# Six SBUF buffers of a four-layer transformer kernel start 128 bytes later

## The chip, the cores and the metric

The kernel runs on one core of one Trainium2 chip. The metric is the device time of one execution in microseconds, the median of several runs.

## The reference

Two blocks of two layers each work on 256 tokens of 1024 features, all in float32. Cut to what matters here:

```
# first block
z = rmsnorm(x, g) @ a_w_in;  q, k, v, q_mem = split(z)       # rope on q and k
x = x + concat(diff_attention(q, k, v), memory_attention(q_mem, mem)) @ a_w_out
x = x + relu(rmsnorm(x, g) @ a_w_up)**2 @ a_w_down
kv = rmsnorm(x, kv_norm) @ w_kv;  z = rmsnorm(x, g) @ b_w_in
x = x + concat(moba_attention(...), memory_attention(...)) @ b_w_out
x = x + relu(rmsnorm(x, g) @ b_w_up)**2 @ b_w_down
x = rmsnorm(x, final_norm)
# second block
h = x + rmsnorm(stick_breaking_attention(rmsnorm(x, g) @ sb_w_qkv) @ sb_w_o, g)
h = h + rmsnorm(conv_ffn(rmsnorm(h, g)), g)                  # up, causal conv of width 3,
h = h + rmsnorm(forgetting_attention(q, k, v, fcum) @ fox_w_o, g)   # gelu(gate) * up, down
h = h + rmsnorm(conv_ffn(rmsnorm(h, g)), g)
```

`fcum` is the running sum of the log of a forget gate, which comes from the product with `w_f`, 16 columns padded to 128.

## The kernel before

The activations lie with features on the partitions: `X` is 128 x 8 x 256, feature tile by token. The work is a list of 18 products, `GEMMS`: `mem_a`, `in_a`, `mem_b`, `out_a`, `up_a`, `down_a`, `in_b`, `out_b`, `up_b`, `down_b`, `in_sb`, `out_sb`, `up_sb`, `down_sb`, `in_fox`, `out_fox`, `up_fox`, `down_fox`. I call the stretch of the trace in which one is computed a stage.

**The weights.** SyncE streams them in units of 128 x 1024 (128 x 768 or 640 in `down_sb` and `down_fox`) into `raw`, a ring of four slots. ScalarE rounds a unit to the float32r type into `w_hi` (L815), VectorE subtracts to get the rest into `w_lo` (L1128). A unit holds up to eight k-tiles of 128 x 128.

**The activations** are split the same way. `h1_hi`, `h1_lo` and `h2_hi`, `h2_lo` hold the normed input of a product (L819 on ScalarE writes hi, L1172 on VectorE writes lo); `a_hi`, `a_lo` hold the hidden layer of an MLP, `o_hi`, `o_lo` the attention output. Every k-tile costs three matmuls of 256 columns, a triple:

```
nc.tensor.matmul(dst, w_hi[:, slot, w], src_hi[:, at + k, :], start=begin, stop=False)   # L497
nc.tensor.matmul(dst, w_hi[:, slot, w], src_lo[:, at + k, :], start=False, stop=False)   # L498
last = nc.tensor.matmul(dst, w_lo[:, slot, w], src_hi[:, at + k, :], start=False,        # L499
```

The first operand of `matmul` after the destination is stationary, loaded by a weight load of its own; the second moves. L467 to L469 in `query_key_tile` are the same triple for the fused projections, L517 to L519 the same for the first tiles of `up_sb` and `up_fox`. Sources: `h2` for `up_a`, `up_b`, `up_sb`, `up_fox` and for the memory tiles in `in_a`; `h1` or `h2` by tile in `in_b` and `in_fox`; `h1` in `in_sb`; `o` for all `out_` and `a` for all `down_` stages. The value columns of the fused projections (L447 to L449) have it the other way round: `h1` is stationary, `w` moves, 512 or 256 columns at a time. The forget gate's product (L729 to L731) has `wf_hi` and `wf_lo` stationary and `h1` moving.

**H** is a work buffer with several uses: attention outputs before their norm, outputs before a post-norm, and in the MLPs `u_buf`, `m_buf` and `gate` are views of it:

```
u_buf = H[:, 0:4, :]
m_buf = H[:, 4:6, :]
gate = H[:, 6:8, :]
```

In `up_sb` and `up_fox`, tile by tile: VectorE scales a bank into `u_buf` (L1226), ScalarE starts `conv_buf` with one tap (L876), GpSimd makes another tap's product in `m_buf` (L1555), VectorE adds a tap (L1232), GpSimd adds `m_buf` (L1561) and, for every pair, multiplies `gate` with it into `prod` (L1566); ScalarE rounds `prod` into `a_hi` (L865), VectorE makes `a_lo` (L1192). `ZM` holds the memory input and later the memory keys, `mv_tok` the memory values, `wf_hi` and `wf_lo` the split of `w_f`.

**Order.** All engines run their own program; counters (semaphores) tie them. For a matmul unit TensorE waits for `lo_ready` of its weights and `tile_out` of the bank it reuses, nothing else in the steady state.

**Where buffers lie.** `sb(name, shape)` gives buffers one after another in the order of the calls, each beginning where the one before ends, small ones rounded up to 32 bytes per partition. Two calls whose result is not kept only take room: `lead_h1`, 48 x 4 = 192 bytes, and `lead_ident`, 192 bytes. Counted from the start of `raw`, `w_hi` begins at 16384, `w_lo` at 32768, `X` at 49152, `h1_hi` at 57536, `h1_lo` at 65728, `h2_hi` at 73920, `h2_lo` at 82112, `H` at 90304, `ZM` at 98496, `mv_tok` at 106688, `wf_hi` at 110784, `wf_lo` at 114880. A tile of 256 tokens is 1024 bytes, a k-tile of weights 512.

Of the kernel before, what the change touches and what calls it, by code (L numbers as in the profile page):

```python
# [22 lines left out]
P = 128  # L23
# [89 lines left out]
def build_program(nc, ins, out):  # L113
# [6 lines left out]
    with ctx:  # L120
        def sb(name, shape, dt=f32):
            return ctx.enter_context(nc.sbuf_tensor(name, shape, dt))
# [10 lines left out]
        h1_hi = sb("h1_hi", [P, KT, TOK], f32r)  # L133
        h1_lo = sb("h1_lo", [P, KT, TOK], f32r)
        h2_hi = sb("h2_hi", [P, KT, TOK], f32r)
        h2_lo = sb("h2_lo", [P, KT, TOK], f32r)
        H = sb("H", [P, KT, TOK])
        ZM = sb("ZM", [P, KT, TOK])
        mv_tok = sb("mv_tok", [P, 2, 2, MEM_W])
        wf_hi = sb("wf_hi", [P, KT, P], f32r)  # L140
        wf_lo = sb("wf_lo", [P, KT, P], f32r)
        sb("lead_ident", [P, 48])
        ident = sb("ident_sb", [P, P])
        ones = sb("ones_sb", [P, TOK])
        rope_c = sb("rope_c_sb", [P, TOK])
# [1544 lines left out]
```

## Time and profile before

| | us |
|---|---|
| median of 3 runs | 1337.02 |
| lowest and highest | 1335.78, 1337.67 |
| the profiled execution's own time | 1337.67 |
| its span, first to last instruction | 1335.9 |

The span is the part of the profiled execution that the trace shows; the time has 1.8 us more around it. The profile's engines are PE (TensorE matmuls), PEld (its weight loads), DVE (VectorE), ACT (ScalarE) and POOL (GpSimd). A matmul's duration runs to its modelled end and overlaps the next one's, so the starts, not the durations, tell how fast they follow each other. PEclk is the TensorE clock granted, 1.00 for full and 0.50 for half.

### The profile page before, as it was taken

How to read it: one execution, taken by the hardware profiler on the slowest of the kernel's cores; microseconds unless marked ns; L12 is line 12 of the kernel's file. 1: busy time of each engine (PE TensorE's matmuls, PEld its weight loads, DVE VectorE, ACT ScalarE, POOL GpSimd, SP SyncE). 2: the span in 40 equal slices, each digit the busy share in tenths (PEclk: the TensorE clock that was granted, in tenths of full speed). 3: DMA queues.
4: the chain of work that ended last, by engine and by line, in shares of the span. 5: the costliest groups of instructions: out<-in, count | busy, mean ns of one | idle time of the engine just before them, and what ended most of it. 6: DMA issues, size and time to landing. Idle time of an engine off the chain costs nothing. (4 is left out here: it accounts for less than half of the span.)

```text
span 1335.9 us, 29554 instructions
## 1 busy us (share of the span) xinstructions
PE 1246.4 (93%) x9952; PEld 1177.5 (88%) x9952; DVE 947.2 (71%) x1545; ACT 734.2 (55%) x1307; POOL 477.9 (36%) x465
## 2 busy tenths in 40 slices
PE   7988999999997999999997889998999999899896
PEld 7977999999985999999885779998979978899896
DVE  6598677656597677545699479997475756899844
ACT  6556554444554555444656566665465556666642
POOL 2231255300022355210222258885130004888711
PEclk9999899999998999999998799999989989999998
DMA  7544365566543456656443225555645433555472
GB/s 273 174 143 127 111 205 189 178 196 204 177 142 96 157 189 192 202 188 190 157 127 111 82 93 179 173 182 151 186 136 174 127 95 112 158 181 171 141 207 85
DMA packets 63287, 212.40 MB, mean 159 GB/s; under 512 B 7793, under 2 KB 8945, under 8 KB 62833
## 3 DMA queue, kind: packets, MB, share of 16 engines
q1 hardware_dynamic: 63216, 211.50, 50.3%
q8 instruction: 39, 0.64, 0.2%
q14 instruction: 32, 0.25, 0.1%
HBM read 207.28 MB, written 1.05 MB: 156 GB/s over the span
## 5 line engine op out<-in xcount | busy, mean ns | idle before, releaser
L1128 DVE TENSOR_TENSOR w_lo<-raw,w_hi 128x1024 fp32r<-128x1024 f32 (+2 forms) x408 | 508.9, 1253 | 144.8 <-ACT w_hi L815 144.8
L815 ACT CAST w_hi<-raw 128x1024 fp32r<-128x1024 f32 (+2 forms) x408 | 408.2, 1004 | 251.6 <-PE bank L499 166.3
L497 PE MATMUL bank<-h_hi,w_hi 128*128 128x256 f32 x1168 | 328.6, 281 | 12.2 <-DVE w_lo L1128 11.3
L498 PE MATMUL bank<-h_lo,w_hi 128*128 128x256 f32 x1168 | 324.0, 277 | 0.0
L499 PE MATMUL bank<-h_hi,w_lo 128*128 128x256 f32 x1168 | 323.9, 277 | 0.0
L1497 POOL TENSOR_TENSOR sumsq<-sumsq,square 128x256 f32<-128x256 f32 x107 | 95.6, 893 | 471.5 <-ACT square L827 287.2
L497 PE MATMUL bank<-a_hi,w_hi 128*128 128x256 f32 x896 | 251.3, 281 | 11.0 <-DVE w_lo L1128 9.3
L498 PE MATMUL bank<-a_lo,w_hi 128*128 128x256 f32 x896 | 250.5, 280 | 0.0
L499 PE MATMUL bank<-a_hi,w_lo 128*128 128x256 f32 x896 | 250.4, 279 | 0.0
L497 PEld LDWEIGHTS bank<-h_hi,w_hi 128*128 128x128 f32 x1168 | 220.2, 189 | 19.3 <-issue 18.6
L499 PEld LDWEIGHTS bank<-h_hi,w_lo 128*128 128x128 f32 x1168 | 220.4, 189 | 0.0
L498 PEld LDWEIGHTS bank<-h_lo,w_hi 128*128 128x128 f32 x1168 | 220.1, 188 | 0.1
L497 PEld LDWEIGHTS bank<-a_hi,w_hi 128*128 128x128 f32 x896 | 170.4, 190 | 12.4 <-DVE w_lo L1128 10.1
L498 PEld LDWEIGHTS bank<-a_lo,w_hi 128*128 128x128 f32 x896 | 170.4, 190 | 0.0
L499 PEld LDWEIGHTS bank<-a_hi,w_lo 128*128 128x128 f32 x896 | 169.8, 190 | 0.0
L467 PE MATMUL bank<-h_hi,w_hi 128*128 128x256 f32 x512 | 147.6, 288 | 0.0
L468 PE MATMUL bank<-h_lo,w_hi 128*128 128x256 f32 x512 | 143.3, 280 | 0.0
L469 PE MATMUL bank<-h_hi,w_lo 128*128 128x256 f32 x512 | 143.1, 280 | 0.0
L1541 POOL TENSOR_TENSOR prod<-H 128x256 f32<-128x256 f32 x64 | 89.2, 1393 | 84.8 <-DVE H L1203 84.8
L467 PEld LDWEIGHTS bank<-h_hi,w_hi 128*128 128x128 f32 x512 | 97.4, 190 | 5.1 <-issue 4.9
L1555 POOL TENSOR_TENSOR H<-H,conv_sb 128x256 f32<-128x256 f32 x88 | 97.1, 1103 | 9.8 <-DVE H L1226 7.7
L469 PEld LDWEIGHTS bank<-h_hi,w_lo 128*128 128x128 f32 x512 | 97.2, 190 | 0.0
(154 smaller groups left out, 2123.6 us busy)
## 6 DMA issues: line engine op xcount, KB each, us to landing
raw<-in_w_up_sb SPq DMA_DIRECT2D x44, 512.0 KB, 3.4
raw<-in_w_up_fox SPq DMA_DIRECT2D x44, 512.0 KB, 3.4
raw<-in_w_up_a SPq DMA_DIRECT2D x32, 512.0 KB, 3.4
raw<-in_w_down_a SPq DMA_DIRECT2D x32, 512.0 KB, 4.7
raw<-in_w_up_b SPq DMA_DIRECT2D x32, 512.0 KB, 3.4
raw<-in_w_down_b SPq DMA_DIRECT2D x32, 512.0 KB, 4.4
raw<-in_w_in_sb SPq DMA_DIRECT2D x24, 512.0 KB, 3.6
raw<-in_w_in_fox SPq DMA_DIRECT2D x24, 512.0 KB, 4.3
```

The source lines that it names most:

```text
L467: nc.tensor.matmul(dst, w_hi[:, slot, w], src_hi[:, k, :], start=k == 0, stop=False)
L468: nc.tensor.matmul(dst, w_hi[:, slot, w], src_lo[:, k, :], start=False, stop=False)
L469: last = nc.tensor.matmul(dst, w_lo[:, slot, w], src_hi[:, k, :], start=False, stop=k == KT - 1)
L497: nc.tensor.matmul(dst, w_hi[:, slot, w], src_hi[:, at + k, :], start=begin, stop=False)
L498: nc.tensor.matmul(dst, w_hi[:, slot, w], src_lo[:, at + k, :], start=False, stop=False)
L499: last = nc.tensor.matmul(dst, w_lo[:, slot, w], src_hi[:, at + k, :], start=False, stop=end)
L815: nc.scalar.copy(w_hi[:, slot, 0:k * P], raw[:, slot, 0:k * P]).then_inc(hi_ready, 1)
L1128: nc.vector.tensor_tensor(w_lo[:, slot, 0:k * P], raw[:, slot, 0:k * P], w_hi[:, slot, 0:k * P].bitcast(f32), ALU.subtract).then_inc(lo_re ...
L1497: nc.gpsimd.tensor_tensor(sumsq[:], sumsq[:], square[:, b, :], ALU.add).then_inc(sum_done, 1)
L1541: nc.gpsimd.tensor_tensor(prod[:, b % 2, :], u_buf[:, b, :], u_buf[:, b, :], ALU.mult).then_inc(prod_ready, 1)
L1555: nc.gpsimd.tensor_tensor(m_buf[:, b % 2, :], u_buf[:, b % 2, :], conv[:, layer, 0, bass.ds(i * 4 + b, 1)].broadcast_to([P, TOK]), ALU.mul ...
```

## The change

One spacer of 128 bytes per partition is put ahead of `h2_lo`, and the later spacer `lead_ident` is made 128 bytes shorter. So `h2_lo`, `H`, `ZM`, `mv_tok`, `wf_hi` and `wf_lo` start 128 bytes later; all buffers ahead of them and all from `ident_sb` on stay. The instructions are the same.

```diff
         h2_hi = sb("h2_hi", [P, KT, TOK], f32r)
+        sb("lead_h2_lo", [P, 32])
         h2_lo = sb("h2_lo", [P, KT, TOK], f32r)
         H = sb("H", [P, KT, TOK])
         ZM = sb("ZM", [P, KT, TOK])
         mv_tok = sb("mv_tok", [P, 2, 2, MEM_W])
         wf_hi = sb("wf_hi", [P, KT, P], f32r)
         wf_lo = sb("wf_lo", [P, KT, P], f32r)
-        sb("lead_ident", [P, 48])
+        sb("lead_ident", [P, 16])
         ident = sb("ident_sb", [P, P])
```

## Rows read from the trace of the kernel before

**Rows 1.** The cores view (span, mean granted clock); busy time from the page.

```profile
core 0: 1335.9 us, clock 0.966
...
PE 1246.4 (93%) x9952; PEld 1177.5 (88%) x9952; DVE 947.2 (71%) x1545; ACT 734.2 (55%) x1307; POOL 477.9 (36%) x465
```

**Rows 2.** Windows: length, busy and (count) PE, PEld, DVE, ACT, POOL; PEclk, DMA.

```profile
164.00:251.00 87.00, 86.70 (x764) 86.45 (x762) 63.54 (x97) 46.26 (x68) 44.12 (x33) 1.00 0.62 195
...
435.00:462.00 27.00, 27.00 (x228) 27.00 (x227) 19.99 (x26) 15.12 (x25) 9.10 (x8) 0.98 0.43 139
...
745.00:772.00 27.00, 26.22 (x205) 25.00 (x205) 10.56 (x10) 13.56 (x27) 5.21 (x7) 0.91 0.44 136
772.00:922.00 150.00, 139.73 (x1127) 134.81 (x1125) 131.69 (x174) 93.90 (x157) 122.03 (x124) 0.98 0.48 150
922.00:981.00 59.00, 57.89 (x478) 57.89 (x479) 28.80 (x33) 30.39 (x46) 5.19 (x7) 0.97 0.68 195
...
1265.00:1336.00 71.00, 57.78 (x481) 56.81 (x481) 32.34 (x42) 28.97 (x47) 9.38 (x11) 0.94 0.48 142
```

**Rows 3.** Timeline (start, length), weight loads, up_a (41 rows) and down_a (42).

```profile
199.89 0.19 PEld L497 LDWEIGHTS bank<-h_hi,w_hi 128*128 128x128 f32 x1
...
204.42 0.19 PEld L498 LDWEIGHTS bank<-h_lo,w_hi 128*128 128x128 f32 x1
...
299.85 0.19 PEld L497 LDWEIGHTS bank<-a_hi,w_hi 128*128 128x128 f32 x1
...
304.49 0.19 PEld L499 LDWEIGHTS bank<-a_hi,w_lo 128*128 128x128 f32 x1
```

**Rows 4.** The same timeline in down_sb (40 rows) and out_b (39 rows).

```profile
949.83 0.19 PEld L498 LDWEIGHTS bank<-a_lo,w_hi 128*128 128x128 f32 x1
...
954.42 0.19 PEld L498 LDWEIGHTS bank<-a_lo,w_hi 128*128 128x128 f32 x1
...
439.93 0.19 PEld L499 LDWEIGHTS bank<-o_hi,w_lo 128*128 128x128 f32 x1
...
444.40 0.19 PEld L498 LDWEIGHTS bank<-o_lo,w_hi 128*128 128x128 f32 x1
```

**Rows 5.** The same timeline, the forget gate's product (23 rows).

```profile
1014.33 0.19 PEld L730 LDWEIGHTS bank<-h_lo,wf_hi 128*128 128x128 f32 x1
...
1016.96 0.19 PEld L731 LDWEIGHTS bank<-h_hi,wf_lo 128*128 128x128 f32 x1
```

**Rows 6.** The same timeline, the value product's 256-wide part in in_a (39 rows).

```profile
43.99 0.19 PEld L448 LDWEIGHTS bank<-w_lo,h_hi 128*128 128x128 f32 x1
...
48.47 0.19 PEld L447 LDWEIGHTS bank<-w_hi,h_hi 128*128 128x128 f32 x1
```

**Rows 7.** Down_sb at half the granted clock: window, then timeline (13 rows).

```profile
924.20:927.20 3.00, 3.00 (x16) 3.00 (x15) 2.33 (x3) 2.24 (x5) 0.62 (x1) 0.50 0.70 183
...
924.46 0.33 PEld L498 LDWEIGHTS bank<-a_lo,w_hi 128*128 128x128 f32 x1
...
927.02 0.33 PEld L498 LDWEIGHTS bank<-a_lo,w_hi 128*128 128x128 f32 x1
```

**Rows 8.** Windows of two successive pairs of tiles in up_sb, columns as in rows 2.

```profile
836.37:842.39 6.02, 5.72 (x48) 5.53 (x49) 5.51 (x8) 3.82 (x7) 5.28 (x6) 1.00 0.56 174
842.39:848.36 5.97, 5.92 (x48) 5.72 (x49) 5.49 (x8) 3.81 (x7) 5.22 (x6) 1.00 0.51 176
```

**Rows 9.** The chain that ended last, within up_sb: start, length, what.

```profile
849.13 0.65 POOL conv_buf L1561
...
850.00 1.45 POOL prod L1566
```

**Rows 10.** Two source lines of VectorE: duration ns min/median/max, first and last start.

```profile
L1354 DVE SCALAR_TENSOR_TENSOR H<-H,subln_s,n_buf x6: 479/480/484, 110.2 to 139.4; 128x256 f32<-128x256 f32 x6
...
L1434 DVE SCALAR_TENSOR_TENSOR X<-X,gains_sb,rstd x8: 471/474/958, 634.7 to 643.1; 128x256 f32<-128x256 f32 x8
```

**Rows 11.** The tile view of H, its last step on GpSimd, columns as in rows 10.

```profile
L1566 POOL TENSOR_TENSOR prod<-H,conv_buf x44: 727/1440/1601, 796.9 to 1263.7; 128x256 f32<-128x256 f32 x44
```

## The prediction

> **What bounds the kernel now.** I read the cores view first: one core, span 1335.9 us, mean granted TensorE clock 0.966 [rows 1]. The page's first part gives the engines: TensorE is busy 93% and its weight loads 88%, VectorE only 71%. The windows by stage then separate two kinds of stage [rows 2]. In up_a, out_b and down_sb TensorE is busy for 86.7 of 87, 27.0 of 27 and 57.9 of 59 us, nearly all of it at the full granted clock: there the time is set by how fast matmuls follow each other (down_a, up_b, down_b, the other out stages and down_fox are of this kind too). In up_sb TensorE is idle for 10 of 150 us, and VectorE (131.7) and GpSimd (122.0) are as good as full; up_fox is the same.
>
> For a change of addresses the busy time says too little, because a matmul's duration in the trace overlaps its neighbours'. The spacing of the starts is what counts. The timeline of weight loads alone (one load per matmul) gives it: first and last row of an unbroken stretch, divided by the number of steps. In up_a 40 steps take 204.42 - 199.89 = 4.53 us, 113.3 ns each, and in down_a 41 steps take 4.64 us, 113.2 ns [rows 3]. The same loop in down_sb takes 4.59 us for 39 steps, 117.7 ns, and in out_b 4.47 us for 38, 117.6 ns [rows 4]; out_sb and down_fox go at that pace too. So one loop, on operands placed alike, has two stable paces 4.4 ns apart. I call them the quick and the slow pace. Which one a stretch has is settled soon after TensorE starts again from a gap.
>
> Two other matmul groups are placed differently. Take addresses as distances from the start of raw. The buffers w_hi and w_lo sit at 0 modulo 512 bytes; all of h1, h2, o and a at 192. In the ordinary loop the moving operand (h, o or a) is therefore 192 ahead of the stationary one (w). In the forget-gate product (L729 to L731) both are at 192, distance 0: 22 steps take 1016.96 - 1014.33 = 2.63 us, 119.5 ns [rows 5]. In the value product (L447 to L449) w moves and h1 is stationary, distance 0 - 192, which is 320 modulo 512: its 256-wide part takes 48.47 - 43.99 = 4.48 us for 38 steps, 117.9 ns [rows 6]. The pace thus seems to hang on where the two operands lie relative to each other, though these groups differ from the loop in other ways as well.
>
> **The change part by part.** No instruction, wait, semaphore or DMA is added or removed. What changes is where six buffers lie: h2_lo, H, ZM, mv_tok, wf_hi and wf_lo each start 128 bytes later, at 320 instead of 192 modulo 512. The second spacer is 128 bytes shorter, so ident_sb and all after it stay. What stays relative is as important: h2_hi, h1, w, a and o are untouched.
>
> *h2_lo on TensorE.* It is the moving operand of the second matmul of each triple (L498, L468, L518) in up_a, up_b, up_sb, up_fox and in part of the fused projections. Its distance from w becomes 320, that of the value product. No row shows that distance in this loop. The cost is bounded from both sides. From above: the whole stream takes the value product's pace. up_a and up_b have 32 tiles of 8 triples each, 512 triples or 1536 matmuls, times 4.4 ns = 6.8 us. If the slow pace is then carried on without a gap into down_a and down_b (8 tiles of 32 k-tiles each, 2 x 768 matmuls), that is another 6.8 us. A nearer value is that only the matmul that reads h2_lo pays: 512 x 4.4 ns = 2.3 us. Nothing is lost if the distance doesn't matter, or if 192 and 320, which are 64 bytes to either side of a multiple of 256, are worth the same. From below: the quick pace is not the floor. Where the granted clock is 0.50 (its 1.2 GHz level) the loop takes 213.3 ns a step, 12 steps in 927.02 - 924.46 = 2.56 us [rows 7]; half of that at the full clock is 106.7, against the 113.3 of [rows 3], so a better distance could give back up to 6.6 ns. On 512 matmuls that is 3.4 us, and on all 1536 of up_a and up_b 10 us. I take the middle between nothing and one in three, 1.2 us, because two of the three matmuls in each triple keep their distance.
>
> *The same in up_sb and up_fox* (44 tiles each): costed at nothing. The two windows of [rows 8] are successive pairs of tiles, 48 matmuls each. The first is at the quick pace for most of its length, the second wholly at the slow one (its TensorE busy time is 5.92 against 5.72 us), and they take 6.02 and 5.97 us. What sets a pair is the chain in [rows 9]: conv_buf on VectorE, conv_buf and prod on GpSimd, a_hi, then the next w_lo. 48 matmuls need 5.44 us quick and 5.65 us slow, so there are at least 0.3 us of cover. Were it gone, the cost would be 2 x 352 x 4.4 ns = 3.1 us for one in three.
>
> *The fused projections.* 32 triples of the memory tiles in in_a, and 64 each in in_b and in_fox, read h2_lo. One in three paying is 160 x 4.4 ns = 0.7 us at most, and these stages have TensorE gaps, so I take nothing.
>
> *H, ZM, mv_tok and wf.* H is read and written by the chain of up_sb and up_fox. Do addresses matter to VectorE? The same form at 128x256 takes 479 to 484 ns when both inputs lie at 192 (H and n_buf, L1354), and 471 at the least with X at 0 and rstd at 64 (L1434) [rows 10]: 8 ns apart. One such step per pair on the chain and 44 pairs give 0.4 us either way. For GpSimd I see only durations that include waiting for VectorE: prod 727 to 1601 ns, median 1440 [rows 11]. With the same 2% on its 0.65 and 1.45 us it would be 44 x 0.042 = 1.8 us either way; I take 0. wf is read by 24 matmuls: at best 24 x (119.5 - 113.3) ns = 0.15 us back, taken as 0. ZM and mv_tok are used by a few tens of small operations, nothing.
>
> The sum: 1.2 us on the profiled execution's 1337.67 us, that is its span of 1335.9 us and 1.8 us around it, or 1338.9. It is the slowest of three; on the median 1337.02 it gives 1338.2 us.
>
> The Trainium skill speaks to this on its page "SBUF — State Buffer", section "Who interferes with whom": TensorE has two independent read ports, one for the moving operand and one for weights, and it and ScalarE never wait on anyone. By that rule the sum is 0. The 119.5 against 113.3 ns of [rows 5] and [rows 3] do not fit it easily, and so I leave it a part of my forecast and not the whole. The same page, in its specifications, says that SBUF works in 16-byte lines; 128 bytes is eight of them, so no access comes to lie across more lines, and no run here shows that.
>
> **The rivals.**
> *The distance counts for the whole stream* (slower). One late read per triple shifts the loads behind it, and the triple settles at the slow pace, as every triple of out_b and down_sb does. It speaks for this that a stretch is wholly quick or wholly slow, never a third of it, and that the value product stays at 117.9. It speaks against it that the value product also switches banks and uses one stationary operand twice. Price: 6.8 us for up_a and up_b, 13.6 us if it carries on to down_a and down_b, giving 1343.8 to 1350.6 us. It decides once the mean spacing in up_a is over 115 ns.
>
> *The moved h2_lo breaks the slow pace, or the starts fall out well* (faster). In four long stretches the slow pace now costs: out_b, out_sb, down_sb and down_fox. Their windows hold 228 + 205 + 478 + 481 = 1392 matmuls [rows 2], of which some 1320 follow at it once each stage has got going: 1320 x 4.4 ns = 5.8 us. Each is entered from a gap, and a start that is a few ns different can fall to the quick pace. All four give 1331.2 us; with the 3.4 us above, 1327.8. Against: none of these four reads h2_lo, so it takes a knock-on, and the three runs lie within 1.9 us, so the paces seem to repeat from run to run. It decides once two of the down and out stages turn quick.
>
> *Nothing at all happens*: 1337.0 us. For it speaks that 192 and 320 lie equally far from 256, and it lies inside the forecast's own case.
>
> **How the numbers follow.** 0.2% is 2.7 us, about what a measurement of this kernel can tell from no change. The forecast's case, between nothing and one matmul in three, spans 1337.0 to 1339.3 us; with a pace or two falling out otherwise in the short stretches its own range is 1334.5 to 1340. I give it 0.42. The whole stream slow: 0.29, plus 0.04 for long stretches turning slow by themselves. Faster, by a better pace or by better starts: 0.25. So faster 0.25, same 0.42, slower 0.33. The range runs from 1330.5 (nearly all four slow stretches turned quick) to 1346.5 (up_a, up_b and half of what may carry on).
>
> **What the profile afterwards would show.** First the spacing in up_a and up_b: 113.3 ns for no effect, about 114.7 for one in three, 117.7 for the rival. Then the same in down_a and down_b, where nothing moved. The pair time in up_sb and up_fox stays at 5.99 us, or H matters. The spacing of the forget-gate product tells by itself whether distance counts: there wf moves from 0 to 384, and only placement changes. DVE and ACT durations stay as they are. The prediction is wrong if up_a's pace moves by more than 2 ns, or if stages whose operands were not moved change pace by themselves and add up to more than 2.7 us.

## The result and the profile after

The changed kernel takes 1347.62 us (median of 6 runs, 1343.56 to 1350.45), the kernel before beside it 1335.02 us (6 runs, 1331.48 to 1337.67). The ratio is 1.0087, with a 95% interval from 1.0066 to 1.0107. It is slower; the forecast was 1338.2 us, and the range ended at 1346.5. The profiled execution of the changed kernel took 1344.47 us, its span is 1342.6 us.

The added spacer moves every line number of the kernel by one: L497 to L499 of before are L498 to L500 here. The windows of the changed kernel's trace, columns as in [rows 2] (up_a, down_a, up_b, down_b, then up_sb and up_fox from their first to their last weight load):

```profile
161.00:251.00 90.00, 89.80 (x761) 89.54 (x760) 64.00 (x97) 45.76 (x67) 43.42 (x33) 1.00 0.58 188
253.00:343.00 90.00, 90.00 (x767) 90.00 (x765) 50.84 (x55) 41.08 (x54) 7.42 (x9) 1.00 0.58 190
462.00:552.00 90.00, 89.79 (x761) 89.53 (x760) 64.07 (x96) 45.91 (x68) 43.42 (x33) 1.00 0.58 189
554.00:645.00 91.00, 90.47 (x766) 90.07 (x765) 42.91 (x42) 36.25 (x42) 8.81 (x9) 1.00 0.60 189
...
790.80:927.40 136.60, 131.65 (x1059) 127.62 (x1059) 122.39 (x163) 87.01 (x143) 112.53 (x112) 0.99 0.46 149
1128.10:1264.80 136.70, 132.22 (x1059) 127.74 (x1059) 122.26 (x163) 87.03 (x143) 110.70 (x112) 0.99 0.46 149
```

Up_a holds 761 matmuls in 90 us where 87 us held 764 before [rows 2], at the same full granted clock and with TensorE busy throughout. So the matmuls follow each other more slowly and nothing else waits. The timeline of weight loads shows it; first and last row of an unbroken stretch in up_a (40 rows), down_a (40), up_b (39) and down_b (39):

```profile
199.90 0.19 PEld L498 LDWEIGHTS bank<-h_hi,w_hi 128*128 128x128 f32 x1
...
204.49 0.19 PEld L498 LDWEIGHTS bank<-h_hi,w_hi 128*128 128x128 f32 x1
...
299.89 0.19 PEld L498 LDWEIGHTS bank<-a_hi,w_hi 128*128 128x128 f32 x1
...
304.48 0.19 PEld L498 LDWEIGHTS bank<-a_hi,w_hi 128*128 128x128 f32 x1
...
499.93 0.19 PEld L500 LDWEIGHTS bank<-h_hi,w_lo 128*128 128x128 f32 x1
...
504.41 0.19 PEld L499 LDWEIGHTS bank<-h_lo,w_hi 128*128 128x128 f32 x1
...
599.92 0.19 PEld L500 LDWEIGHTS bank<-a_hi,w_lo 128*128 128x128 f32 x1
...
604.40 0.19 PEld L499 LDWEIGHTS bank<-a_lo,w_hi 128*128 128x128 f32 x1
```

That is 4.59 us for 39 steps in up_a and in down_a, 117.7 ns, and 4.48 us for 38 in up_b and down_b, 117.9 ns, against 113.3 and 113.2 in [rows 3]. In down_a and down_b, where no operand was moved, the pace is just as slow.

Where it begins is plain from the rows at the step from out_a to up_a, which has no gap. Start times of consecutive loads in the changed kernel:

```profile
160.97 0.19 PEld L499 LDWEIGHTS bank<-o_lo,w_hi 128*128 128x128 f32 x1
161.09 0.19 PEld L500 LDWEIGHTS bank<-o_hi,w_lo 128*128 128x128 f32 x1
161.20 0.19 PEld L498 LDWEIGHTS bank<-h_hi,w_hi 128*128 128x128 f32 x1
161.31 0.19 PEld L499 LDWEIGHTS bank<-h_lo,w_hi 128*128 128x128 f32 x1
161.43 0.19 PEld L500 LDWEIGHTS bank<-h_hi,w_lo 128*128 128x128 f32 x1
161.54 0.19 PEld L498 LDWEIGHTS bank<-h_hi,w_hi 128*128 128x128 f32 x1
161.66 0.19 PEld L499 LDWEIGHTS bank<-h_lo,w_hi 128*128 128x128 f32 x1
161.78 0.19 PEld L500 LDWEIGHTS bank<-h_hi,w_lo 128*128 128x128 f32 x1
```

Up to the load of the first h_lo the steps are 0.11 us with an occasional 0.12 (113 and 114 ns in the trace's own starts, which these rows round); from the first matmul that reads h2_lo on they are 113 to 120 ns, 117.4 on average over the next 18. The stream was quick, and the moved operand turned it slow at once.

Stage by stage, from one stage's first weight load to the next one's, up_a took 91.3 us instead of 88.1, down_a 91.2 instead of 87.8, up_b 91.4 instead of 87.7 and down_b 95.5 instead of 92.1: 13.8 us in the four together (for a down stage the next first load is that of the values that follow). The two spans differ by only 6.7 us, because other stages took less than in the trace of before: down_sb 2.0 us, out_fox 1.7, the stretch from in_fox's first query tile to out_fox 1.1, out_b 0.7 and several less. The medians, 12.6 us apart, are the better measure.

What did not change: up_sb and up_fox. They hold the moved h2_lo too, and went slow (117.6 and 117.7 ns a step instead of 114.6 and 114.2), but take 136.6 and 136.7 us as against 136.5 and 136.7 before: VectorE (122.4 us) and GpSimd (112.5) are nearly full in that window, and their chain hides it. H moved, and its users in the changed kernel kept their durations (tile view and source lines, columns as in [rows 10] and [rows 11]):

```profile
L1355 DVE SCALAR_TENSOR_TENSOR H<-H,subln_s,n_buf x6: 478/480/485, 109.7 to 139.0; 128x256 f32<-128x256 f32 x6
...
L1567 POOL TENSOR_TENSOR prod<-H,conv_buf x44: 727/1442/1604, 809.3 to 1270.5; 128x256 f32<-128x256 f32 x44
```

The forget gate's product, which the prediction named as a test of its own, did change: its stationary wf moved and nothing else of it. The mean of its 22 steps is 118.8 ns instead of 119.6 (2.61 us instead of the 2.63 of [rows 5]).

### The profile page after: what moved, and what is told of

The parts are those of the page before. It is cut to its first block and busy times, and to the rows that moved or that the text cites. A ratio compares the mean times of both kernels' runs of the same rounds, so it can differ in the third digit from the quotient of the medians.

```text
span 1342.6 us, 29554 instructions
## 1 busy us (share of the span) xinstructions
PE 1258.1 (94%) x9952; PEld 1189.0 (89%) x9952; DVE 949.3 (71%) x1545; ACT 732.5 (55%) x1307; POOL 478.1 (36%) x465
## 5 line engine op out<-in xcount | busy, mean ns | idle before, releaser
L498 PE MATMUL bank<-h_hi,w_hi 128*128 128x256 f32 x1168 | 332.3, 285 | 6.6 <-DVE w_lo L1129 4.0
L499 PE MATMUL bank<-h_lo,w_hi 128*128 128x256 f32 x1168 | 329.3, 282 | 0.0
L500 PE MATMUL bank<-h_hi,w_lo 128*128 128x256 f32 x1168 | 327.6, 281 | 0.0
L498 PE MATMUL bank<-a_hi,w_hi 128*128 128x256 f32 x896 | 253.5, 283 | 10.9 <-DVE w_lo L1129 9.5
L499 PE MATMUL bank<-a_lo,w_hi 128*128 128x256 f32 x896 | 252.7, 282 | 0.0
L500 PE MATMUL bank<-a_hi,w_lo 128*128 128x256 f32 x896 | 252.7, 282 | 0.0
L498 PEld LDWEIGHTS bank<-h_hi,w_hi 128*128 128x128 f32 x1168 | 220.0, 188 | 13.9 <-issue 12.9
L500 PEld LDWEIGHTS bank<-h_hi,w_lo 128*128 128x128 f32 x1168 | 221.4, 190 | 0.0
L499 PEld LDWEIGHTS bank<-h_lo,w_hi 128*128 128x128 f32 x1168 | 220.3, 189 | 0.1
L498 PEld LDWEIGHTS bank<-a_hi,w_hi 128*128 128x128 f32 x896 | 170.1, 190 | 12.6 <-DVE w_lo L1129 10.6
L500 PEld LDWEIGHTS bank<-a_hi,w_lo 128*128 128x128 f32 x896 | 172.3, 192 | 0.0
L499 PEld LDWEIGHTS bank<-a_lo,w_hi 128*128 128x128 f32 x896 | 170.8, 191 | 0.0
L1542 POOL TENSOR_TENSOR prod<-H 128x256 f32<-128x256 f32 x64 | 89.2, 1393 | 91.2 <-DVE H L1204 91.2
L469 PEld LDWEIGHTS bank<-h_lo,w_hi 128*128 128x128 f32 x512 | 96.4, 188 | 0.0
```

The costliest lines, as they stand in the source:

```text
L469: nc.tensor.matmul(dst, w_hi[:, slot, w], src_lo[:, k, :], start=False, stop=False)
L1542: nc.gpsimd.tensor_tensor(prod[:, b % 2, :], u_buf[:, b, :], u_buf[:, b, :], ALU.mult).then_inc(prod_ready, 1)
```

## The experiments

Theory 1: the distance of the moving operand from the stationary w, modulo some power of two, decides whether a stream can go quick; h2_lo's new distance can't. Theory 2: any shift changes the starts by some ns, and the pace falls anew by chance. Theory 3: it is the other five buffers. In the edits below the spacers are written in bytes per partition; where a compensating spacer stands behind the moved buffer, all that follows is at its old place modulo 512. Each ratio is against the kernel before, run beside it on the same chip; the chips' medians of it differ by 2 us.

The table has what each trace shows, the mean step in ns of weight loads in a stage (mean of all steps of 100 to 130 ns in it), so that the verdicts can be compared in one place. The distance is that of h2_lo from w, moving less stationary, modulo 512; in e8 it is h2_hi that lies at 320.

```
kernel          moved                 h2_lo dist  up_a  down_a  up_b  down_b out_a out_b out_sb out_fox down_sb down_fox
before          -                     192        113.4  113.3  113.6  113.3  113.4 117.8 117.8  113.4   117.3   117.7
changed         h2_lo..wf +128        320        117.8  117.8  117.8  117.8  113.4 113.4 117.8  113.3   113.8   117.3
e13 (the same)  h2_lo..wf +128        320        117.8  117.8  117.8  117.8  113.4 113.4 113.4  113.3   117.3   113.5
e1              H..wf +128            192        113.6  113.3  113.3  113.3  117.8 113.4 117.8  113.4   113.8   117.7
e2              h2_lo +128            320        117.8  113.3  117.8  117.8  113.4 113.5 117.8  113.3   113.4   117.3
e3              h2_lo +256            448        113.3  113.3  113.4  113.3  113.5 113.5 113.4  117.7   117.7   113.5
e4              h2_hi, h2_lo +128     320        117.8  117.8  117.8  117.8  113.4 113.5 113.4  113.3   117.3   117.8
e8              h2_hi +128            192        117.7  113.4  117.7  113.4  117.8 113.4 117.8  113.4   113.4   113.4
e7              h2_lo +384            64         117.8  117.8  117.8  113.3  113.6 113.4 113.4  113.4   113.8   113.4
e9              h2_lo +64             256        119.2  113.4  119.2  113.4  113.5 113.4 113.5  113.3   113.8   113.8
e10             h2_lo +192            384        118.9  113.3  118.9  113.3  113.5 113.3 113.5  113.3   117.3   117.3
e11             all moving +32        224        118.3  118.3  118.3  118.3  118.3 118.3 118.4  118.3   118.3   118.3
e12             all moving -32        160        117.4  117.3  118.6  118.7  118.6 117.3 117.3  117.3   118.5   117.5
e5              changed + odd matmul  320        117.8  113.4  117.8  113.4  113.4 117.8 113.4  113.4   117.3   117.7
e14 (the same)  changed + odd matmul  320        117.8  113.4  117.8  113.4  117.8 113.5 113.5  117.7   117.4   113.4
e6              before + odd matmuls  192        113.6  117.6  113.6  117.6  117.6 117.8 117.8  117.3   117.6   113.8
```

**e1: move all but h2_lo.** The 128-byte spacer stands behind h2_lo instead of ahead of it.

```diff
         h2_lo = sb("h2_lo", [P, KT, TOK], f32r)
+        sb("lead_H", [P, 32])
         H = sb("H", [P, KT, TOK])
-        sb("lead_ident", [P, 48])
+        sb("lead_ident", [P, 16])
```

> H, ZM, mv_tok and wf start 128 bytes later, h2_lo stays where it was. Theory 1 (the distance of the moving h2_lo from w sets the pace): up_a, down_a, up_b and down_b keep 113.3 ns a step, and the time is that of before within 0.3%. Theory 2 (any shift makes the starts fall out anew): some long stages change pace, within 5 us either way, no pattern. Theory 3 (the other five buffers do it): +10 to +14 us and up_a at 117.7 to 118 ns.

Measured: ratio 1.0016 (0.9998 to 1.0033), 1333.03 us against 1331.33; up_a 113.6 ns, the other three 113.3. Theory 3 falls.

This run also speaks to a rival that the other edits leave open. They move the moving operand and never w, so the place of the moving operand by itself would explain them as well as its distance from w. In the forget gate's product of e1 the moving h1 stays and the stationary wf shifts by 128 bytes, to distance 384. First and last of 23 rows:

```profile
1012.43 0.19 PEld L731 LDWEIGHTS bank<-h_lo,wf_hi 128*128 128x128 f32 x1
...
1015.04 0.19 PEld L732 LDWEIGHTS bank<-h_hi,wf_lo 128*128 128x128 f32 x1
```

That is 2.61 us for 22 steps, 118.6 ns, against 119.5 in [rows 5]. The difference is small but repeats: by the trace's own starts the mean is 118.8 ns in all five traces with wf moved (e1, the changed kernel, e13, e5, e14) and 119.4 to 119.9 in the other eleven. The place of the stationary operand counts too, and the values fit those of the ordinary loop: 118.9 ns at 384 (e10), 119.2 at 256 (e9).

**e2: move h2_lo alone.**

```diff
+        sb("lead_h2_lo", [P, 32])
         h2_lo = sb("h2_lo", [P, KT, TOK], f32r)
+        sb("lead_H", [P, 96])
         H = sb("H", [P, KT, TOK])
```

> h2_lo alone starts 128 bytes later; a second spacer of 384 bytes brings H and all that follows back to the same place modulo 512. Theory 1: up_a, down_a, up_b and down_b at 117.7 ns a step, +10 to +14 us, as in the changed kernel. Theory 3: as before within 0.3%. Theory 2: up_a quick in some runs.

Measured: ratio 1.0082 (1.0052 to 1.0113), 1343.19 us against 1331.33. h2_lo alone accounts for the loss: the ratio is that of the changed kernel within the intervals. The trace has up_a, up_b and down_b slow, but down_a quick, which theory 1 had not expected. First and last row in up_a (40 rows), then in down_a (42):

```profile
199.88 0.19 PEld L501 LDWEIGHTS bank<-h_hi,w_lo 128*128 128x128 f32 x1
...
204.47 0.19 PEld L501 LDWEIGHTS bank<-h_hi,w_lo 128*128 128x128 f32 x1
...
299.85 0.19 PEld L501 LDWEIGHTS bank<-a_hi,w_lo 128*128 128x128 f32 x1
...
304.50 0.19 PEld L500 LDWEIGHTS bank<-a_lo,w_hi 128*128 128x128 f32 x1
```

4.59 us for 39 steps is 117.7 ns, 4.65 us for 41 is 113.4 ns.

**e3: 256 bytes instead of 128.** As e2, spacers of 256 and 256 bytes.

```diff
+        sb("lead_h2_lo", [P, 64])
         h2_lo = sb("h2_lo", [P, KT, TOK], f32r)
+        sb("lead_H", [P, 64])
```

> h2_lo alone starts 256 bytes later (distance 448 modulo 512), the rest as before modulo 512. If what counts is the distance modulo 256, this is the kernel before: 113.3 ns in up_a, same time within 0.3%. If it is modulo 512 or the place itself, up_a is slow, +10 us. Theory 2: no pattern.

Measured: ratio 1.0007 (0.9993 to 1.0021), 1332.53 us. A shift twice as large does nothing: up_a is at 113.3 ns. That is the strongest evidence against theory 2, and it points to a period of 256 bytes. First and last of 41 rows in up_a, 4.53 us for 40 steps:

```profile
199.87 0.19 PEld L500 LDWEIGHTS bank<-h_lo,w_hi 128*128 128x128 f32 x1
...
204.40 0.19 PEld L501 LDWEIGHTS bank<-h_hi,w_lo 128*128 128x128 f32 x1
```

**e4: h2_hi and h2_lo together.**

```diff
+        sb("lead_h2_hi", [P, 32])
         h2_hi = sb("h2_hi", [P, KT, TOK], f32r)
         h2_lo = sb("h2_lo", [P, KT, TOK], f32r)
+        sb("lead_H", [P, 96])
```

> h2_hi and h2_lo both start 128 bytes later (all three matmuls of a triple at distance 320), the rest as before modulo 512. If distance 320 is bad by itself, up_a is at 117.7 ns or slower, +10 us or more. If only the mixture of two distances within a triple is bad, up_a is quick at 113.3 ns and the time is that of before.

Measured: ratio 1.0069 (1.0043 to 1.0095), 1342.54 us. Up_a and up_b at 117.8 ns: distance 320 is bad by itself, and it costs no more with all three matmuls at it than with one.

**e5: break the stream ahead of down_a and down_b.** The changed kernel, with one plain float32 matmul of the ones tile ahead of both.

```diff
+            keep_warm(ones, 1)
             gemm("down_a", a_hi, a_lo)
...
+            keep_warm(ones, 1)
             gemm("down_b", a_hi, a_lo)
```

> The changed kernel with one plain float32 matmul of the ones tile (as in keep_warm) on TensorE ahead of down_a and ahead of down_b. If those stages were slow only because the slow pace of up_a and up_b was carried over without a gap, the odd matmul lets them start anew and they go at 113.3 ns: 6.5 us less than the changed kernel, 1337 to 1339 us on a chip where the kernel before takes 1331 to 1333. If something else of the change slows them, they stay at 117.8 ns and the time at that of the changed kernel.

Measured: ratio 1.0068 (1.0043 to 1.0093), 1340.45 us against 1331.86; down_a and down_b at 113.4 ns, up_a and up_b still at 117.8. The slow pace of the down stages was carried over; the size of that in the time was left to e13 and e14.

**e6: the same odd matmul in all out and down stages of the kernel before.** An attempt at a faster kernel.

```diff
                     for s in range(done, body * nk):
+                        if part_way and s == 1:
+                            keep_warm(ones, 1)
...
+                breaks = name[:4] in ("out_", "down")
+                if breaks:
+                    trip(0, part_way=True)
                 if g["trips"] > 1:
-                    with pe.Fori(1 if peeled else 0, g["trips"]) as i:
+                    with pe.Fori(1 if peeled or breaks else 0, g["trips"]) as i:
```

> The kernel before with the same odd matmul after the first unit of every out and down stage. If it resets the pace as the sum of squares does in up_a and up_b, out_b, out_sb, down_sb and down_fox all go at 113.3 to 113.5 ns, up to 5 us less than before, at 0.2 us each for the matmul: 1327 to 1331 us. If the pace falls anew by chance, half of the stages stay slow and the time is that of before within 0.2%.

Measured: ratio 1.0103 (1.0079 to 1.0127), 1343.24 us. Both expected outcomes were wrong: it is slower than before. The odd matmul turns quick streams slow. In down_a, loads around it:

```profile
251.23 0.19 PEld L500 LDWEIGHTS bank<-a_lo,w_hi 128*128 128x128 f32 x1
251.34 0.19 PEld L501 LDWEIGHTS bank<-a_hi,w_lo 128*128 128x128 f32 x1
251.45 0.30 PEld L564 LDWEIGHTS bank<-ones_sb 128*128 128x128 f32 x2
251.78 0.19 PEld L499 LDWEIGHTS bank<-a_hi,w_hi 128*128 128x128 f32 x1
252.00 0.19 PEld L500 LDWEIGHTS bank<-a_lo,w_hi 128*128 128x128 f32 x1
252.11 0.19 PEld L501 LDWEIGHTS bank<-a_hi,w_lo 128*128 128x128 f32 x1
252.23 0.19 PEld L499 LDWEIGHTS bank<-a_hi,w_hi 128*128 128x128 f32 x1
252.35 0.19 PEld L500 LDWEIGHTS bank<-a_lo,w_hi 128*128 128x128 f32 x1
252.47 0.19 PEld L501 LDWEIGHTS bank<-a_hi,w_lo 128*128 128x128 f32 x1
```

Steps of 0.11 ahead of it and mostly 0.12 after it, and the rest of the 768 matmuls stays at that. The matmuls right behind the odd one are slow in all eight out and down stages; out_b and down_fox were slow ahead of it already. Seven stages end slow; down_fox turns quick only after a wait of 1.9 us further on. So the pace after an interruption isn't drawn at random, but neither does an interruption as such make it quick. In up_a and up_b the sum of squares, a plain float32 matmul as well, was followed by the quick pace in every trace in which h2 lies at 192, though four of these stages were slow ahead of it. What tells the two apart wasn't tried.

**e7: h2_lo 384 bytes later**, distance 64. As e2 with `[P, 96]` ahead of h2_lo and `[P, 32]` behind it.

> h2_lo alone starts 384 bytes later: distance 64 modulo 512, the rest as before modulo 512. If the distance counts modulo 256 this equals the changed 320, up_a at 117.7 ns, +7 to +13 us. If it counts modulo 512 the run may be quick, at the time of before.

Measured: ratio 1.0121 (1.0103 to 1.0139), 1346.56 us; up_a and up_b at 117.8 ns. Distance 64 is like 320, and 448 like 192: again 256 is the period.

**e8: h2_hi alone**, `[P, 32]` ahead of h2_hi and `[P, 96]` ahead of h2_lo.

> h2_hi alone starts 128 bytes later (distance 320 in two matmuls of each triple), h2_lo stays at 192. If any one matmul at 320 is enough to keep the slow pace, up_a is at 117.7 ns and +7 to +14 us. If it hangs on the h_lo matmul alone, the one after which w_lo is loaded, up_a stays at 113.3 ns and the time at that of before.

Measured: ratio 1.0117 (1.0089 to 1.0144), 1345.07 us; up_a and up_b at 117.7 ns. Either operand of the triple suffices. The profiled execution (1336.75 us), with down_a and down_b quick, is the shortest of the four measured and 8.3 us below the median. Two slow down stages in the other executions would be 6.8 of these; that is not shown, since they have no trace.

**e9 and e10: h2_lo 64 and 192 bytes later**, distances 256 and 384. As e2 with `[P, 16]` and `[P, 112]`, and with `[P, 48]` and `[P, 80]`.

> h2_lo alone starts 64 bytes later: distance 256, which is 0 modulo 256, the rest as before modulo 512. The forget gate's product at distance 0 goes at 119.5 ns, so up_a and up_b are expected at 117.7 to 119.5 ns: +7 to +15 us. If only the distances 64 and 320 were bad, up_a is at 113.3 ns and the time that of before.

> h2_lo alone starts 192 bytes later: distance 384, 128 modulo 256. Not yet seen in any run. If 192 modulo 256 is the only distance with a quick pace, up_a is at 117.7 ns or slower, +7 to +14 us; if 128 is far enough from 0 as well, it is as before.

Measured: ratios 1.0050 (1.0029 to 1.0071) and 1.0067 (1.0041 to 1.0093), 1339.73 and 1341.2 us. The step in up_a is 119.2 and 118.9 ns, slower still than at 320, but down_a and down_b are quick in both traces. e9's up_a, 39 rows, 4.53 us for 38 steps:

```profile
199.91 0.19 PEld L500 LDWEIGHTS bank<-h_lo,w_hi 128*128 128x128 f32 x1
...
204.44 0.19 PEld L499 LDWEIGHTS bank<-h_hi,w_hi 128*128 128x128 f32 x1
```

**e11 and e12: all moving operands 32 bytes further, or 32 bytes nearer.** All buffers behind `lead_h1` shift along.

```diff
-        sb("lead_h1", [P, 48])
+        sb("lead_h1", [P, 56])      # e11; [P, 40] in e12
```

> lead_h1 is 224 instead of 192 bytes: all of h1, h2, o and a lie at distance 224 from w. If quick needs just 192, the whole kernel goes slow: some 7700 matmuls at +4.4 ns, of which the up_sb and up_fox ones are hidden, +20 to +25 us. If the whole quarter from 192 to 256 is good, same time; if the best distance is above 192, the slow stages of before turn quick, up to 5.8 us less.

> lead_h1 is 160 bytes: all moving operands at distance 160. The same three outcomes as for 224: +20 to +25 us if quick needs just 192, same time if there is a broad good zone, up to 5.8 us less if the best distance is below 192.

Measured: ratios 1.0168 (1.0149 to 1.0187) and 1.0174 (1.0157 to 1.0191), 1355.36 and 1355.77 us, 22 us more than before. Not one long stage is quick in either; 32 bytes off is already off. Since h1 moved as well, the value product shows the same from the other side: h1 is stationary there and w, which moves, kept its place. It is at 116.7 ns a step in e11 and at 119.9 to 120.0 in e12, and at 113.3 or 117.8 in every other trace. e11's down_a, 39 rows, 4.50 us for 38 steps, 118.4 ns:

```profile
299.92 0.19 PEld L499 LDWEIGHTS bank<-a_hi,w_lo 128*128 128x128 f32 x1
...
304.42 0.19 PEld L498 LDWEIGHTS bank<-a_lo,w_hi 128*128 128x128 f32 x1
```

**e13 and e14: the changed kernel, and e5, once more on one chip**, with no edit.

> The changed kernel once more, unaltered, beside the next one. up_a and up_b are at 117.8 ns again, whatever the starts do. If the slow pace always carries over into down_a and down_b, both are slow again; if that falls by chance, one or both are at 113.4 ns in this trace, and the single times spread over some 7 us. Ratio to before 1.006 to 1.010.

> The changed kernel with the odd matmul ahead of down_a and down_b, once more. down_a and down_b at 113.4 ns again. If in the changed kernel both always go slow, this one is 6.5 us faster than it on the same chip; if only one does on average, about 3 us.

Measured: ratios 1.0104 (1.0078 to 1.0130) and 1.0064 (1.0042 to 1.0085), 1345.61 and 1340.97 us. In e13 both down stages are slow again, in e14 both are quick again. The odd matmuls take 4.6 us off the median, less than the 6.5 us that two quick down stages would give; the single times of both kernels spread over 9 to 12 us, so the executions differ among themselves, and the medians don't measure the carry-over closely. e14's down_a, 41 rows, 4.53 us for 40 steps:

```profile
299.90 0.19 PEld L500 LDWEIGHTS bank<-a_hi,w_lo 128*128 128x128 f32 x1
...
304.43 0.19 PEld L498 LDWEIGHTS bank<-a_hi,w_hi 128*128 128x128 f32 x1
```

## Why the prediction was wrong

**The step that failed** is the size taken for h2_lo on TensorE, 1.2 us where the four stages of up_a to down_b took 13.8 us more: "the middle between nothing and one in three, 1.2 us, because two of the three matmuls in each triple keep their distance". The triple doesn't pay in thirds. One matmul at distance 320 keeps the whole stream at the slow pace, and e4 (all three), e2 (one) and e8 (the other two) cost the same 4.4 ns per step of all. For up_a and up_b that is 3.3 and 3.7 us in the trace, 7.0 together; the rival had computed 6.8. The other 6.8 us are in down_a and down_b, which the forecast put at nothing. The prediction had the evidence at hand and weighed it too lightly: a stretch is wholly quick or wholly slow, never a third of it.

**The rival** "the distance counts for the whole stream" is what happened, with its second half: 6.8 us for the up stages and as much again carried over into down_a and down_b, 1343.8 to 1350.6 us. Measured was 1347.6. That its price fitted is in part luck: it was taken from the value product at 320, which turned out to be no measure of this loop (below), and at 256 and 384 a step costs 5.9 and 5.6 ns and not 4.4. Its point of decision, a spacing over 115 ns in up_a, was met. It had 0.29 where the forecast's own case had 0.42, and the range was cut at half of the carry-over. The upper bound of the unknown cost was thus worked out and then left outside the range. The range's ends are also not the sums they are said to be: 1337.0 with 6.8 and half of 6.8 is 1347.2 and not 1346.5, and with all four slow stretches turned quick it is 1331.2, above the 1330.5 given for nearly all.

**Carry-over.** It is shown by the odd matmul in e5 and e14 (four down stages quick), and by both traces of the changed kernel (four slow). Even the kernel before has it: out_b is slow, up_b's first 50 steps go at 117.7 ns, and after the sum of squares the rest goes at 113.3. So a pace can pass a border of stages, which the prediction's "settled soon after TensorE starts again from a gap" leaves out. It is not a rule: with h2_lo at 320 or 64, down_a or down_b began quick in e2 and e7, and with h2_lo at 256 or 384, and with h2_hi at 320, both did.

For h2_lo alone at 320 or 64 the traces tell the cases apart ahead of the border. Take the last 40 triples of an up stage, by the starts in ns: ahead of the six stages that stay slow (the changed kernel, e13, e2's up_b, e7's up_a) every triple takes 352 to 355 ns; ahead of the two that turn quick (e2's up_a, e7's up_b) triples of about 350 and 357 alternate. The four up stages of e5 and e14 are all of the even kind, so without the odd matmul their down stages would be expected to stay slow. What makes one kind or the other, and why the other placements don't hand the pace on, stays open.

**The grounds for a rule of distance.** The forget gate's 119.5 ns at distance 0 [rows 5] pointed the right way: e9 gives the ordinary loop 119.2 ns at distance 256. The value product [rows 6] didn't, for it has both paces: in the changed kernel's in_a it goes at the quick one, with neither operand moved. First and last of 45 rows there:

```profile
44.85 0.19 PEld L449 LDWEIGHTS bank<-w_lo,h_hi 128*128 128x128 f32 x1
...
49.84 0.19 PEld L448 LDWEIGHTS bank<-w_hi,h_hi 128*128 128x128 f32 x1
```

That is 4.99 us for 44 steps, 113.4 ns. With roles exchanged distance 320 can be quick, which the ordinary loop never was there, so that row was no measure of the loop at 320. The prediction's other test, the forget gate's spacing, came out for the distance (e1).

**What was right.** Up_sb and up_fox hid their part: in both traces the windows are the same length to 0.1 us. H, ZM, mv_tok and wf cost nothing that a measurement can tell (e1, at most 0.33%). The Trainium skill's rule on the page "SBUF — State Buffer", section "Who interferes with whom", that TensorE never waits on anyone and reads moving and stationary data through independent ports, would have made the sum 0. The 117.7 against 113.3 ns, from one operand's address alone (e2 and e3), is a cost of placement which that rule leaves no room for as far as TensorE's own two reads are concerned. Whether the reads themselves collide isn't shown, nor that TensorE waits for another engine. Better starts (the faster rival) did occur in the changed kernel's trace, in out_b and down_sb, where the two stages took 0.7 and 2.0 us less; e13, the same kernel, has out_b quick but down_sb slow.

**What stays open.** The mechanism behind the distance. That two reads of TensorE collide where they fall on the same part of a 256-byte pattern would fit the period and the slowest pace at 256, but not by itself the slow pace at 128 and 64 modulo 256, and no run here looks inside. Why the value product can be quick at 64 modulo 256 and the loop can't is open too. Open also are the distances that were not tried, and what decides the pace at a start.

## What to carry to other kernels

Where matmuls follow each other without a gap, measure the spacing of the starts, not the busy time, and compare the same loop across stages: two stable values for the same instructions mean that something decides which the instruction list doesn't show. Then the place of a buffer in SBUF is a parameter like any other, to be kept with a comment and a spacer when buffers are added, since 32 bytes on all moving operands cost this kernel 22 us of 1333. And when a trace shows that a cost is all or nothing, the middle between all and nothing is the value least likely to be measured.

## What the runs showed of the hardware

- In the ordinary loop (128x128 weights, 256 moving columns, weight load and matmul alternating) the step depends on where the moving operand lies relative to the stationary one, and 256 bytes further is the same again: of the distances tried, 113.3 ns is reached at 192 and 448 only; 64 and 320 give 117.7 to 117.8, 224 gives 118.3, 384 gives 118.9, 256 gives 119.2, 160 gives 117.3 to 118.7 (e1 to e4, e7 to e12). At 448, 64, 384 and 256 only h2_lo was moved, one matmul in three.
- Moving only the stationary operand changes the step as well: 119.6 to 118.8 ns in the forget gate's product (e1). With w moving and h1 stationary the step also hangs on placement, but 113.3 ns is reached there at 320 (the changed kernel), where the ordinary loop doesn't reach it (e4).
- At a distance where 113.3 is reached, 117.7 is stable too: the same loop kept either through hundreds of matmuls, and which one it takes is settled at a start, an interruption or a change of operands, and in the out stages, down_sb and down_fox it differs between two traces of one kernel (the changed kernel and e13, e5 and e14).
- One operand of three at a bad distance is enough for the whole stream, and the slow pace can outlast it into a stage with good placement (both down stages in the changed kernel and in e4), until an odd matmul breaks it (e5, e14). The same odd matmul in a quick stream leaves it slow (e6: down_a and down_b, 113.4 to 117.8 ns).
- 128 bytes on H's place made no difference to the two operations on VectorE and GpSimd that were looked at (medians of 480 and 1442 ns against 480 and 1440).
